# Gates of a PEER expert sweep stored and read for eight experts at a time, in two buffers

## The reference

```
q = (h @ w_query) -> 8 heads, two halves;  s1, s2 = halves @ sub_keys
top 16 of each, then top 16 of the 256 sums -> expert index, gate = softmax(score)
u = expert_down[index];  a = gelu(h . u);  y += (gate * a) * expert_up[index]
```

## Time and profile before

| | us |
|---|---|
| median of three executions | 1637.77 |
| the profiled execution | 1633.12 |
| its span in the trace | 1631.3 |
| TensorE busy | 1545.5 (95%) |
| VectorE busy | 1232.0 (76%) |
| ScalarE busy | 598.9 (37%) |
| GpSimd busy | 496.8 (30%) |
| DMA moved | 373.48 MB |

### The profile page before, as it was taken

The page is one execution under the profiler, slowest core; times in us unless marked ns, Lnnn a source line. Parts: engine busy times, 40 slices in busy tenths (PEclk is TensorE's granted clock), DMA queues, the critical chain, the costliest instruction groups (busy, mean ns, idle before and its releaser), DMA issues.

```text
span 1631.3 us, 22488 instructions
## 1 busy us (share of the span) xinstructions
PE 1545.5 (95%) x8493; PEld 1358.1 (83%) x8493; DVE 1232.0 (76%) x2262; ACT 598.9 (37%) x996; POOL 496.8 (30%) x326
## 2 busy tenths in 40 slices
PE   6998999989999999997998899999999999999995
PEld 5876887768889989996777777999999999999995
DVE  7435765357999999983666666888888888888874
ACT  5214554252322346561333333333333333333332
POOL 0000000045673830001111112455455455545510
PEclk9997999999999999998999999999999999999998
DMA  6210000233322558889888888999999999999951
GB/s 272 103 52 1 1 1 1 96 127 123 123 72 72 167 150 301 331 303 372 280 291 286 285 283 267 315 370 339 348 356 354 350 355 349 349 358 355 350 196 52
DMA packets 145724, 373.48 MB, mean 229 GB/s; under 512 B 11440, under 2 KB 75568, under 8 KB 142416
## 3 DMA queue, kind: packets, MB, share of 16 engines
q1 hardware_dynamic: 98624, 197.30, 35.6%
q0 software_dynamic: 37200, 138.56, 23.4%
q10 hardware_dynamic: 9792, 36.18, 6.0%
HBM read 333.72 MB, written 38.27 MB: 228 GB/s over the span
## 4 chain that ended last, share of the span: by engine, by line
PE 64%; DVE 25%; DMA 6%; ACT 2%; issue 2%; POOL 1%; SPq 0%; DVEq 0%; ACTq 0%
PE bank L1161 28%; PE bank L1421 26%; DMA u_raw<-up 5%; PE bank L1272 3%; PE bank L1298 2%; DVE oh L1078 2%; DVE oh L1081 2%; DVE gp L1083 2%; DVE gp L1086 1%; PE bank L1284 1%; DVE cand L1016 1%; DVE d_lo L1067 1%; DMA g_e<-gates_dram 1%; DVE ti L990 1%; DVE work L991 1%
## 5 line engine op out<-in xcount | busy, mean ns | idle before, releaser
L1161 PE MATMUL bank<-h_hi,d_hi 128*128 128x384 f32 x1024 | 348.3, 340 | 7.4 <-POOL d_lo L439 4.4
L1161 PE MATMUL bank<-h_lo,d_hi 128*128 128x384 f32 x1024 | 344.9, 337 | 0.0
L1161 PE MATMUL bank<-h_hi,d_lo 128*128 128x384 f32 x1024 | 344.8, 337 | 0.0
L478 POOL DMA_INDIRECT p_in<-rows,p_row x128 | 159.8, 1248 | 411.8 <-DVE p_dot L1105 197.6
L1421 PE MATMUL bank<-u_hi,w_hi_e 128*128 128x512 f32 x768 | 240.6, 395 | 31.9 <-DVE w_lo_e L1132 31.0
L1062 DVE TENSOR_TENSOR u_lo<-u_raw,u_hi 128x1024 fp32r<-128x1024 f32 x128 | 156.7, 1225 | 113.1 <-ACT u_hi L678 112.9
L1421 PE MATMUL bank<-u_lo,w_hi_e 128*128 128x512 f32 x768 | 237.8, 391 | 0.0
L478 POOL DMA_INDIRECT p_in<-up,p_row x128 | 167.3, 1307 | 230.6 <-DVE xt L1111 113.9
L1421 PE MATMUL bank<-u_hi,w_lo_e 128*128 128x512 f32 x768 | 237.4, 390 | 0.0
L1161 PEld LDWEIGHTS bank<-h_hi,d_hi 128*128 128x128 f32 x1024 | 192.9, 188 | 12.5 <-POOL d_lo L439 5.2
L678 ACT ACTIVATE u_hi<-u_raw 128x1024 fp32r<-128x1024 f32 x128 | 135.3, 1057 | 169.0 <-DMA u_raw<-up 85.8
(11 more groups left out here) (221 smaller groups left out, 2293.2 us busy)
## 6 DMA issues: line engine op xcount, KB each, us to landing
d_raw<-down SPq DMA_DIRECT2D x128, 512.0 KB
u_raw<-up SPq DMA_DIRECT2D x128, 512.0 KB
gates_dram<-ev ACTq DMA_DIRECT2D x12, 2048.0 KB, 7.2
g_e<-gates_dram SPq DMA_DIRECT2D x32, 768.0 KB, 8.8
w_raw<-wts SPq DMA_DIRECT2D x9, 2048.0 KB, 8.1
act_dram<-f_act ACTq DMA_DIRECT2D x56, 192.0 KB, 4.9
a_e<-act_dram SPq DMA_DIRECT2D x56, 192.0 KB, 5.2
xt<-x_in SPq DMA_DIRECT2D x4, 512.0 KB, 6.2
```

What stands on the lines that cost most here:

```text
L478: pool.indirect_dma_start(out=p_in[n % GR][:], out_offset=None, in_=rows if kind == "D" else up.rearrange("n p d -> (n p) d"), in_offset=b ...
L1161: m = nc.tensor.matmul(out, a, b, start=(n == 0 and j == 0), stop=(n == last and j == 2))
```

## The change

GB goes from 4 to 8. So there are 16 batches (NGB) in place of 32, a batch is 1,536 KB in place of 768 KB, and the twelve pieces that one partition reads for a batch are 1,024 bytes in place of 512. There are two buffers `g_e` in place of three: 24,576 bytes of a partition in place of 18,432, so `nf` and `squares` move up by 6,144 bytes. The load of batch n waits for the products of batch n-2 (before: n-3). Before the loop two batches are loaded in place of three (eight and eight blocks; before three times four), and in the loop a batch is loaded at e % 8 == 5, batch e // 8 + 1, from batch 2 on. The stores of the gates keep their form: a partition's part of a token group is one contiguous run of 16 KB either way.

```diff
-GB = 4
+GB = 8
...
-    g_e = [sb(f"g_e{i}", [P, NTG, GB, TG]) for i in range(3)]
+    g_e = [sb(f"g_e{i}", [P, NTG, GB, TG]) for i in range(2)]
...
-                if n >= 3:
-                    sp.wait_ge(S("w_mul"), (n - 2) * GB)
-                sp.dma_start(g_e[n % 3][:].rearrange("p i k t -> p i (k t)"), gates_dram[:, :, n])\
-                  .then_inc(S(f"g_loaded{n % 3}"), 16)
+                if n >= 2:
+                    sp.wait_ge(S("w_mul"), (n - 1) * GB)
+                sp.dma_start(g_e[n % 2][:].rearrange("p i k t -> p i (k t)"), gates_dram[:, :, n])\
+                  .then_inc(S(f"g_loaded{n % 2}"), 16)
...
-            load_gates(2)
             for e in range(DR, NK):
...
-                if e % GB == 2 and e // GB + 2 < NGB:
-                    load_gates(e // GB + 2)
+                if e % GB == 5 and 2 <= e // GB + 1 < NGB:
+                    load_gates(e // GB + 1)
...
-                    dve.wait_ge(S(f"g_loaded{n % 3}"), 16 * (n // 3 + 1))
+                    dve.wait_ge(S(f"g_loaded{n % 2}"), 16 * (n // 2 + 1))
...
-                V.tensor_tensor(a_v, a_v, g_e[n % 3][:, :, e % GB], ALU.mult).then_inc(S("w_mul"), 1)
+                V.tensor_tensor(a_v, a_v, g_e[n % 2][:, :, e % GB], ALU.mult).then_inc(S("w_mul"), 1)
```

## The result

The changed kernel takes 1665.39 us (median of 4 runs, 1661.40 to 1670.34) against 1637.03 for the kernel before (4 runs, 1635.08 to 1640.35): ratio 1.0164, interval 1.0143 to 1.0186. It is 28 us slower. The forecast was 1645, in a range up to 1657: the direction was right, the size far too small, and the time lies outside the range.

What follows compares the result with a forecast made beforehand. TensorE, busy 95% of the span, was taken as the bound, so only waits reaching it cost. Start +0.7 and first stage +6.7 gave +7.4 us on a median of 1637.8: 1645 us, range 1633 to 1657.

Steps and rivals of the forecast that it cites:

- (1): Stores and VectorE's product: no change expected, with 2% allowed each way on the product, under 1 us in the stage.
- (4): First stage, six batches: 4.1 us of gaps for eight blocks against 3.0, six times +1.1, +6.7 us.
- (5): New waits for freed buffers and later batches: always free or far ahead, no case of a late batch seen.
- (6): Second stage: no gap in TensorE, so nothing taken; 14 us if the cover of the loads went.
- Part (2): One load of gates in 1,024-byte pieces: 356 GB/s taken, 4.4 us a batch, 1.7 us more than now.
- Part (3): Start of the sweep: gates 0 +1.7 us, bytes behind them -1.0, so +0.7 us, between -0.5 and +2.7.
- first term: First stage, behind each batch: next u arrives after 7.3 us, 3.2 more than the 4.1 allowed.
- the high end: First stage: 5.4 us load, gathers adding 1.3 us at the new place, 6.4 us for eight blocks, +20 us.
- second term: First stage, the four blocks without a batch: 0.9 us of gaps caused by the gathers stays.
- Rival (A): First stage: half clock after each of six gaps, 1.7 us each, 10 us on top, 1655 us; chance 0.15.
- Rival (B): First stage: gaps in the other four blocks shrink to about 0.2 us, 3.4 for eight blocks, 1641 us; chance 0.23.
- Rival (C): First stage: a load's existence costs, not its length; u arrives under 6.0 us, 1632 us, faster; chance 0.17.

Runs made afterwards that it cites:

- at6: Changed kernel with its load of gates one block later (e % 8 == 6 in place of 5): 1656.50 us, ratio 1.0100 to the kernel before.
- none: Changed kernel without loads of gates in the loop or VectorE's wait for batches from 2 on (result wrong): 1622.63 us, ratio 0.9896.
- pairs: Kernel before, batches of four, with four buffers and two batches loaded one behind the other at e % 8 == 5: 1670.19 us, ratio 1.0185.
- warm: Changed kernel with 24 unused matmuls added on TensorE before the waits of blocks 13, 21, 29, 37, 45 and 53: 1654.18 us, ratio 1.0090.
- nogather: Changed kernel with all 256 picks moved to the second stage, second stage overloaded: 1643.10 us, ratio 1.0029.
- actq: Changed kernel with loads of gates from batch 2 on issued by ScalarE (e % 8 == 2) instead of SP: 1655.88 us, ratio 1.0099.
- the halves kernel: Changed kernel with each batch from 2 on loaded in two DMAs of 768 KB, at e % 8 == 2 and 6: 1636.10 us, ratio 0.9975.
- swap_after: Changed kernel; ScalarE rounds block e's product before u of e+1, VectorE takes w_lo_e before u_low of e+1: 1621.90 us, ratio 0.9891.

## Why the prediction was wrong

**The place and the mechanism were right.** The first 56 blocks, a u stuck behind one long load, six gaps before blocks 13, 21, ..., 53, nothing in the second stage (614.5 us either way), nothing in the new waits, the products or the stores: all as parts (1), (4), (5) and (6) said. Part (2) held too: with 1,024-byte pieces alone in the queue the rate was 360 GB/s for the 356 taken. That is nearer to my value than to the 8% saving that I had estimated from the Trainium skill's figures (DMA: Bandwidth & Descriptors, section Why small descriptors are slow), which comes to about 315 GB/s. Against the 291 and 307 GB/s measured with 512-byte pieces the gain is 17 to 24%.

**Part (3), the start,** forecast +1.7 and -1.0: measured +1.7 and -0.8. A half clock behind the 1.91 us gap there (+1.6) was not foreseen, and could not be from the kernel before, where a gap of 1.93 us at this place had none. It came in seven of the eight profiles of batches of eight that have this gap.

**Part (4) failed, in its first term.** "Behind the batch the next u arrives after 5.6 + 1.7 = 7.3 us": it was 9.6, and the gaps near 5 in place of 3.2. I added the extra transfer time to the old arrival. Even without gathers a u needs 8.0 us. The new place adds the gathers' 1.6 us; moving the load back by one block (`at6`) takes 1.4 us off. My reading of the rest is that the old load of 2.7 us lay in part in time in which the queue had nothing to do, such as the idle DMA from 824 to 826 us in `none`, and that the longer one has no such cover; it is argued and not shown, and `pairs`, where 0.7 us of burst made 0.2 of delay, does not bear out a simple sum. I had this second part as "one of 0.52 MB at 404 GB/s adds 1.3 us", but only in the high end, though I had seen that they fall beside the new place. Its second term was wrong as well: the 0.9 us of the other four blocks are not the gathers' own, as `none` shows with 3.2 us in the whole stage. In the changed kernel the three gaps beyond the six long ones sum to 2.1 us, not 5. Two readings of the rows were off without moving the sum: there are ten of those other gaps and eight behind gates, not 11 and seven (10.8 us stands), and the two blocks that bound the arrival last 8.45 us and not 8.2, so that a u has 4.4 us and not 4.1. An arrival of 9.6 us therefore makes gaps near 5 and not 5.5.

**Rival (A), the clock, was true and got 0.15.** I priced it at 10 us (1.7 each); it cost 2.3 each, 13.8, shown by `warm`. The forecast treated a gap of 3.2 us as just short of the only example. That was an error of its own, and does not follow from the gap being 1.8 us too short: in `at6` and `nogather` the clock fell behind gaps of 2.4 to 3.4 us as well, eight of eight, so at the gap of the forecast too it would have cost six times 1.6 us or more, which is what rival (A) had. The longer gap only made it dearer. The gaps' own +14.4 and the clock's +13.8 make the 28. The high end had +20 from gaps, A had +10, and I let the range leave out both together. The Trainium skill's rule on waits for a DMA that re-throttle TensorE in every round (TensorE: Matmul & The Clock Gate, section HAM oscillation) agrees with this trace: all six gaps of 4.4 to 6.5 us were followed by the half clock. It is not so for every wait: the 18 gaps of up to 1.9 us of the kernel before had none, and neither had one of 2.3 us in `nogather` and one of 2.7 in each of `warm` and `actq`.

**Rival (B)** was right on one term: the gaps in the other four blocks shrank, to 0.35 us for eight blocks (2.1 us in six rounds) where it had 0.2. Its time, 1641, kept the arrival of 7.3 us and fell with it. **Rival (C)** falls: u arrives after 9.6 us and not under 6.0. Larger pieces in no longer a burst, the halves kernel, gave 0.25%.

What stays open: why a u needs 8.0 us behind the gates with no gather about, 0.7 more than the forecast's sum.

## What to carry to other kernels

Before two loads are made one, ask what stands behind them in the queue, when that is due after its issue, and whether the shorter load was hidden in idle queue time: here 1.7 us more of load made u 2.6 us later at the old place (5.6 to 8.2) and 4.0 at the new one. Price a gap of TensorE and the lower clock that follows it as one thing: here that was 1.6 us behind gaps of 2.4 to 3.2 us and 2.3 behind gaps of some 5. And where an engine's order makes block e wait for an operand of block e+1, mend the order first: in the kernel before that is worth 33 us by the medians, more than leaving out every load of the loop would bring there (18).

## What the hardware showed that was not expected

A load of 1.5 MB issued from another engine's queue delays a u issued 4 us behind it by as much as one ahead of it in the same queue (mean arrival 9.6 us in both). The queue gave no protection here; whether it would for a u issued at the same time, no run shows. And cutting the batch finer than in two hardly helped: twelve loads of 768 KB cost 15.0 us of gaps, 24 of 384 KB 16.3, and 36 of 256 KB 12.4, each in a single profile, and the medians, 1636.10, 1638.55 and 1636.25 us, do not follow the sizes.

The length of a gap alone does not decide whether the clock falls. A gap of 1.91 us was followed by a clock of 0.79 and one of 1.93 us by 1.00, at the same place of the changed kernel and the one before. Of three gaps of 2.7 us (`warm`, `actq`, `swap_after`) it was one that was followed by a fall. What decides it no run here shows.
